# The last expert pair joins the overflow row: both reach their tokens through TensorE, in two parts

## What is computed

```python
pg = softmax(t @ w_rg + b_rg); p_top, g_idx = top_k(pg, 1)          # one group of four
pe_top, e_idx = top_k(softmax(logits of that group), 2)             # two experts of it
w = p_top * pe_top / sum(pe_top)
act = silu(t @ w_gate[e]) * (t @ w_up[e])
y = sum over the two experts e of w[e] * (act @ w_down[e])
x = x + gate * y                                                    # gate: context or latent
```

## Time and profile before

| | us |
|---|---|
| median of 3 runs (lowest, highest) | 1567.03 (1565.42, 1567.63) |
| profiled execution | 1564.47 |
| its span | 1562.7 |
| TensorE busy | 1432.7 |
| VectorE busy | 765.5 |
| ScalarE busy | 324.1 |
| mean granted TensorE clock | 0.962 of full |

### The profile page before, as it was taken

One profiled execution on the slowest core, in us unless ns is written; L12 is line 12 of the kernel. 1 busy time (PEld: TensorE's weight loads), 2 busy tenths in 40 slices (PEclk: granted clock), 3 DMA queues, 4 the chain that ended last, 5 costly groups with the idle time before them and its releaser, 6 DMA issues. The chain is left out here.

```text
span 1562.7 us, 17939 instructions
## 1 busy us (share of the span) xinstructions
PE 1432.7 (92%) x6537; PEld 740.9 (47%) x6537; DVE 765.5 (49%) x1849; ACT 324.1 (21%) x705; POOL 85.7 (5%) x97
## 2 busy tenths in 40 slices
PE   5998998999688999899999999989998998989975
PEld 2335535444255443366666666445443446454432
DVE  1324205553566544576666666036545455156434
ACT  1105304111223111421111111032112125031101
POOL 0000010000210001000000000010001010100001
PEclk9999999999889999899999999999999999989997
DMA  9989968899895998745555554556998730059995
GB/s 353 386 314 364 387 238 323 334 424 422 321 368 210 418 422 351 263 135 175 174 175 175 175 177 157 212 208 237 422 423 341 301 115 1 0 214 401 423 423 221
DMA packets 152276, 436.84 MB, mean 280 GB/s; under 512 B 6944, under 2 KB 63104, under 8 KB 123136
## 3 DMA queue, kind: packets, MB, share of 16 engines
q1 hardware_dynamic: 136816, 396.93, 66.7%
q10 hardware_dynamic: 11920, 26.24, 4.4%
q0 software_dynamic: 3456, 12.58, 2.3%
HBM read 414.20 MB, written 21.53 MB: 279 GB/s over the span
## 5 line engine op out<-in xcount | busy, mean ns | idle before, releaser
L1001 PE MATMUL bank<-gate_up_weights,hT_gathered 128*64 128x512 f32 (+1 forms) x1280 | 256.4, 601 | 15.4 <-SPq L540 14.5
L839 PE MATMUL bank<-panel,hT 128*128 128x512 f32 x384 | 168.8, 599 | 4.9 <-DMA panel<-in_ret_w_in 4.0
L1001 PEld LDWEIGHTS bank<-gate_up_weights,hT_gathered 128*64 128x64 f32 (+1 forms) x1280 | 82.7, 133 | 181.5 <-issue 181.0
L1015 PE MATMUL bank<-down_weights,actT 128*64 128x512 f32 (+1 forms) x640 | 138.5, 603 | 2.5 <-ACT actT L2144 1.7
L1425 DVE SCALAR_TENSOR_TENSOR ada_sums<-panel,cond_columns,ada_sums 128x384 f32<-128x384 f32 x224 | 121.2, 611 | 0.0
L839 PEld LDWEIGHTS bank<-panel,hT 128*128 128x128 f32 x384 | 73.7, 192 | 94.7 <-issue 89.0
L650 PE MATMUL bank<-panel,hT 128*128 128x512 f32 x240 | 107.6, 607 | 3.4 <-DVE hT L1240 2.5
L986 PE MATMUL bank<-h_hi,P 128*128 128x512 f32 x216 | 94.7, 439 | 2.8 <-DVE h_lo L1614 2.7
L986 PE MATMUL bank<-h_lo,P 128*128 128x512 f32 x216 | 87.8, 406 | 0.0
L650 PE MATMUL bank<-panel,oT 128*128 128x512 f32 x192 | 84.3, 595 | 1.3 <-ACT oT L2053 1.3
L2131 ACT ACTIVATE silu<-bank 128x256 f32<-128x256 f32 x36 | 13.9, 385 | 321.6 <-PE bank L1001 321.6
(11 more groups left out here) (330 smaller groups left out, 1929.1 us busy)
## 6 DMA issues: line engine op xcount, KB each, us to landing
gate_up_weights<-in_gate_up_halves SPq DMA_DIRECT2D x148, 1024.0 KB, 13.6
down_weights<-in_down_rows SPq DMA_DIRECT2D x74, 1024.0 KB, 13.6
panel<-in_w_ada SPq DMA_DIRECT2D x27, 2048.0 KB
panel<-in_w_ada SPq DMA_DIRECT2D x16, 1536.0 KB
ada_panel_third<-in_w_ada SPq DMA_DIRECT2D x9, 2048.0 KB
y_by_slot<-y_rows ACTq DMA_DIRECT2D x32, 512.0 KB, 8.2
panel<-in_ret_w_in SPq DMA_DIRECT2D x16, 1024.0 KB
panel<-in_attn_w_qkv SPq DMA_DIRECT2D x6, 2048.0 KB
```

Of the source, the lines that this page charges most:

```text
L839: last = PE.matmul(ps[t][:], hT[:, k, t * 128:(t + 1) * 128], panel[f % 2][:, k, :], start=k == 0, stop=k == KD - 1)
L1001: last = PE.matmul(ps[2][width * s:width * s + width, :], hg[:, j, k, width * s:width * s + width], gu_ring[w][:, 2 * k // KD, :, k % (KD ...
L1015: last = PE.matmul(ps[6 + half][width * s:width * s + width, :], actT[:, c, width * s:width * s + width], dn_ring[w][:, c, half * 512:half ...
```

## The change

- Row 7 (the last pair) is no longer stored and fetched. Its table of slots times weights is made by `weigh_pair`, transposed by TensorE behind row 7's gate-up, and `hot_table` makes of it the weight of each slot (a sum over tokens) and a 0/1 table of tokens. y is multiplied by the slot's weight in `weighted_row`. The overflow row does the same with its own table.
- y of both rows is split in a high part (ScalarE, rounded to the fp32r type) and a low part (VectorE, the difference), and `pe_last_rows` multiplies each with the 0/1 table in fp32r, summing four products in PSUM.
- Fetches wait for rows 0 to 6 alone. Fetches 1, 3, 5 share one buffer, 2 and 4 another, so fetch 3 waits for take 1, 4 for take 2, 5 for take 3. All six takes stand in `last_row`.
- The first QKV panel has a region of its own; `pe_broadcast` uses transposes; the last adds and norm steps are ordered anew; some semaphores are merged; ScalarE starts a layer only when all sums of the last are done.

The core of the diff:

```diff
     pe_row:
         last.then_inc(sem("row_gateup"), 1)
+        if q == PAIRS - 1:
+            pe.wait_ge(sem("row_weights"), 2 * l + 1)
+            pe_table_T().then_inc(sem("row_PT"), 1)
         if not last_row:
             pe_row_gather(pe, l, q + 1, 0)
         else:
-            pe.wait_ge(sem("unit_weights"), l + 1)
+            pe.wait_ge(sem("row_weights"), 2 * l + 2)
+            pe.wait_ge(sem("row_hot"), 2 * l + 1)
             last = pe_table_T()
...
+    def pe_last_rows(pe, l):
+        pe.wait_ge(sem("row_y_lo"), 3 * l + 1)
+        for t in range(TILES):
+            for half in range(2):
+                o = slice(half * 512, half * 512 + 512)
+                for part in (y_hi7, y_lo7):
+                    PE.matmul(ps[2 * t + half][:], hot7[:, t * 128:(t + 1) * 128], part[:, o],
+                              start=part is y_hi7, stop=False)
+        for t in range(TILES):
+            for half in range(2):
+                o = slice(half * 512, half * 512 + 512)
+                if t == 0:
+                    pe.wait_ge(sem("row_y_lo"), 3 * l + 2 + half)
+                PE.matmul(ps[2 * t + half][:], hot8[:, t * 128:(t + 1) * 128], y_hi8[:, o], start=False, stop=False)
+                PE.matmul(ps[2 * t + half][:], hot8[:, t * 128:(t + 1) * 128], y_lo8[:, o], start=False, stop=True)\
+                    .then_inc(sem("unit_sum"), 1)
...
+        def hot_table(l, q):
+            n = 2 * l + q - (PAIRS - 1) + 1
+            dve.wait_ge(sem("row_PT"), n)
+            step(V.tensor_reduce(slot_weight(q), ps[4][:, 0:T], AX.X, ALU.add))
+            V.tensor_scalar(hots[q - (PAIRS - 1)][:], ps[4][:, 0:T], 0.0, None, ALU.is_gt).then_inc(sem("row_hot"), 1)
...
         def last_row(l):
             n = ROWS * l + PAIRS
-            weigh(0, slice(0, 4), "unit_weights")
+            weigh(0, slice(0, 4), "row_weights")
             dve.wait_ge(sem("row_y"), 2 * n)
             step(V.scalar_tensor_tensor(grow[:], gdiff[:], latent[:, PAIRS:ROWS], moe_gate[:, 0, :], ALU.mult, ALU.add))
+            hot_table(l, PAIRS)
+            take(l, 0)
+            take(l, 1)
+            take(l, 2)
+            dve.wait_ge(sem("row_y_hi"), 3 * l + 1)
+            V.tensor_tensor(y_lo7[:], ybuf[:, 1, :], y_hi7[:].bitcast(F), ALU.subtract).then_inc(sem("row_y_lo"), 1)
             dve.wait_ge(sem("row_silu"), n + 1)
             dve.wait_ge(sem("row_actT"), n)
             V.tensor_tensor(act[:], ps[2][:, FE:2 * FE], silu[:], ALU.mult).then_inc(sem("row_act"), 1)
+            take(l, 3)
+            take(l, 4)
             dve.wait_ge(sem("y_stored0"), 16 * 4 * (l + 1))
+            weighted_row(n, PAIRS, 0, ybuf[:, 0, :])
+            weighted_row(n, PAIRS, 1, ybuf[:, 0, :])
             for half in range(2):
-                take(l, half)
                 o = slice(half * 512, half * 512 + 512)
-                dve.wait_ge(sem("row_down"), 2 * n + half + 1)
-                V.tensor_tensor(ybuf[:, 0, o], ps[6 + half][:], grow[:, o], ALU.mult).then_inc(sem("row_y"), 1)
-            take(l, 2)
-            take(l, 3)
+                dve.wait_ge(sem("row_y_hi"), 3 * l + 2 + half)
+                V.tensor_tensor(y_lo8[:, o], ybuf[:, 0, o], y_hi8[:, o].bitcast(F), ALU.subtract).then_inc(sem("row_y_lo"), 1)
+            take(l, 5)
...
     ScalarE, row:
+            if q == PAIRS:
+                e.wait_ge(sem("y_used"), 2 * TILES * l + 1)
+                e.wait_ge(sem("row_y"), 2 * n)
+                S.activation(y_hi7[:], ybuf[:, 1, :], ACT.Copy).then_inc(sem("row_y_hi"), 1)
             e.wait_ge(sem("row_gateup"), n + 1)
...
     GpSimd, combine:
             pool.wait_ge(sem("y_stored0"), 16 * 4 * (l + 1))
-            pool.wait_ge(sem("y_stored1"), 16 * 4 * (l + 1))
+            pool.wait_ge(sem("y_stored1"), 16 * 3 * (l + 1))
             for i in range(2 * TILES):
-                if i == 4:
-                    pool.wait_ge(sem("y_used"), 2 * TILES * l + 1)
-                elif i == 5:
-                    pool.wait_ge(sem("row_gateup"), ROWS * (l + 1))
+                if i == 1:
+                    pool.wait_ge(sem("row_gateup"), ROWS * l + PAIRS)
+                elif i == 2:
+                    pool.wait_ge(sem("row_hT"), 2 * (ROWS * l + PAIRS) + 2)
+                elif i > 2:
+                    pool.wait_ge(sem("y_used"), 2 * TILES * l + i - 1)
...
     SyncE, start:
-        load_next(f)
+        sp.dma_start(first_qkv[:], qkv_w[0, :, :, 0:512]).then_inc(sem("first_qkv_landed"), 16)
...
     pe_broadcast:
-            last = PE.matmul(ps[bank][:, q * 128:(q + 1) * 128],
-                             mods[:, v * KD + 4 * half + q, c:c + 1].broadcast_to([128, 128]), ident,
-                             start=True, stop=True)
+            last = PE.transpose(ps[bank][:, q * 128:(q + 1) * 128],
+                                mods[:, v * KD + 4 * half + q, c:c + 1].broadcast_to([128, 128]), ident)
...
     attention, squares:
-                    dve.wait_ge(sem("qkv_sb"), 9 * a + 3 * i + t + 1)
+                    dve.wait_ge(sem("qkv_sb"), 9 * a + max(3 * i + t + 1, TILES if l == 0 else 0))
```

More of the change, by code:

```diff
@@ L156, in build_trunk @@
     keep("small_place", [3 * FE])
+    lpart_at = top[0]
     lpart = keep("logit_parts", [T])
@@ L182, in build_trunk @@
     (prob, probT), dn_end = region(("prob", [2, 896]), ("probT", [2, 896]), start=dn2_at)
+    assert dn_end <= dn2_at + 2 * size([2, D])
+    (first_qkv,), dn_end = region(("first_qkv_panel", [KD, 512]), start=dn2_at)
     assert dn_end <= dn2_at + 2 * size([2, D])
@@ L225, in build_trunk @@
     tmp_row = tmp[:].rearrange("p a n -> p (a n)")
-    ytok = [tmp_row, ybuf[:, 1, :], hgt[:], hg_rows[:, 1, :], tmp_row, hg_rows[:, 0, :]]
+    ytok = [tmp_row, hg_rows[:, 1, :], hgt[:], hg_rows[:, 1, :], hgt[:], hg_rows[:, 1, :]]
+    Y_BUFFER = (0, 1, 2, 1, 2, 1)
+    Y_TURN = (1, 3, 2)
+    (hot7,), hot_end = region(("pair_hot", [T], R), start=mix0 + 2 * size([TILES, D]))
+    (hot8,), _ = region(("unit_hot", [T], R), start=lpart_at)
+    hots = (hot7, hot8)
+    (y_lo8, y_lo7), _ = region(("unit_y_lo", [D], R), ("pair_y_lo", [D], R), start=base + size([TILES, D]))
+    (y_hi7,), _ = region(("pair_y_hi", [D], R), start=tmp_at)
+    (y_hi8,), _ = region(("unit_y_hi", [D], R), start=base + size([D]))
     ident, tri, iota = kb[:, 0:128], kb[:, 128:256], kb[:, 256:384]
@@ L262, in build_trunk @@
         kind = l % 3
-        first_panel["mix", l] = len(panels)
+        first_panel["mix", l] = len(panels) - (l == 0)
         prj_base[l] = prj
         if kind == 0:
-            panels += [("attn", l, i) for i in range(5)]
+            panels += [("attn", l, i) for i in range(1 if l == 0 else 0, 5)]
             prj += 5 * TILES
@@ L670, in project_k @@
             for k in range(lo, hi):
-                last = PE.matmul(ps[QKV_BANKS[0][t]][:], hT[:, k, t * 128:(t + 1) * 128], panel[f % 2][:, k, :],
+                last = PE.matmul(ps[QKV_BANKS[0][t]][:], hT[:, k, t * 128:(t + 1) * 128], first_qkv[:, k, :],
                                  start=k == 0, stop=k == KD - 1)
@@ L1164, in _ @@
                                  start=True, stop=True)
-        last.then_inc(sem("normf_ps"), 1)
+        last.then_inc(sem("vectors_ps"), 1)
     def mod_col(v, k, c):
@@ L1732, in row @@
                 o = slice(half * 512, half * 512 + 512)
-                dve.wait_ge(sem("row_down"), 2 * n + half + 1)
-                V.tensor_tensor(ybuf[:, q % 2, o], ps[6 + half][:], grow[:, o], ALU.mult).then_inc(sem("row_y"), 1)
+                if q == PAIRS - 1:
+                    weighted_row(n, q, half, ybuf[:, 1, :])
+                else:
+                    dve.wait_ge(sem("row_down"), 2 * n + half + 1)
+                    V.tensor_tensor(ybuf[:, q % 2, o], ps[6 + half][:], grow[:, o], ALU.mult).then_inc(sem("row_y"), 1)
                 if half == 0 and q < PAIRS:
@@ L1822, in tail @@
                 final(0)
-            take(l, 5)
-            mean_square(n, 1)
-            if l + 1 == depth:
                 units_in(l, 2, 0)
+                mean_square(n, 1)
                 units_in(l, 2, 1)
@@ L2146, in row @@
                 if 1 <= l < depth - 1:
-                    e.wait_ge(sem("unit_PT_sb"), l + 1)
+                    e.wait_ge(sem("gate_rows"), l)
                     e.dma_start(gate_rows.rearrange("v c (k f) -> k (v c) f", f=128), mpan[0:KD, :].rearrange("p (g f) -> p g f", f=128))\
                         .then_inc(sem("gate_rows_stored"), 16)
+                for half in range(2):
+                    o = slice(half * 512, half * 512 + 512)
+                    e.wait_ge(sem("row_y"), 2 * n + half + 1)
+                    S.activation(y_hi8[:, o], ybuf[:, 0, o], ACT.Copy).then_inc(sem("row_y_hi"), 1)
                 return
             row_turned(l, q + 1)
+            if q == PAIRS - 1:
+                return
             e.wait_ge(sem("row_y"), 2 * n + 2)
```

74 lines of the change are left out of this document (47 added, 27 removed).

## The result

| | before | after |
|---|---|---|
| median of 4 runs, us (lowest, highest) | 1566.22 (1563.51, 1567.63) | 1594.24 (1591.58, 1595.98) |
| profiled execution, us | 1564.47 | 1591.58 |
| its span, us | 1562.7 | 1589.8 |
| mean granted TensorE clock | 0.962 | 0.951 |

The account below looks back on a forecast made before the run. TensorE, busy 92% of the span, was taken as the bound, with the change in stretches where it is not fed. Terms 29.4 + 1.0 − 2.1 = +28.3 us gave 1592.8 profiled, 1595.3 median; range 1574 to 1604.

Parts of the forecast that it names:

- U behind T: From overflow row's gate-up matmuls ending (T) to VectorE starting to add its sums (U): 21.8, 19.4, 20.8, 18.0 us.
- Act behind the table and three takes: Overflow row on VectorE: act ends at T+7.4 instead of T+1.0, so down matmuls start 6.3 us later, at T+8.3.
- Fetch 3, then 5: Layer ends: fetch 3 issued T+4.6, landing in 5.2 us; fetch 5 waits for take 3, issued T+11.4.
- Then fetch 5 decides: Layer ends: without the slow clock first sums come at T+16.3, but fetch 5 and take 5, last before U, set U.
- those sums end before U+1.3, so 0: ScalarE's later loads and x-scaling now wait for all sums: costs 0, else up to 1 us a layer.
- Layer 3's weights: Wait for layer 3's weights: one store leaves, three fetches enter; between −1.2 and +2.5 us, taken +1.8.
- End of layer 3: Final norm after U: two takes leave VectorE's path, saving 2.4 us; 8.6 − 2.4 = +6.2.
- Start and broadcasts: Gate broadcasts by transposes, taken −1.5 us, and first QKV panel's earlier load, taken −0.6; together −2.1.
- (a): Second fetches land early, clock stays up: U is T+18.0 everywhere, +20.3 us, about 1587; chance 0.20.
- (b): Last fetch takes 9.7 us in layers 0 to 2, beside panel loads: +35 us, 1602; chance 0.10.
- (c): Overflow row's table built before T, takes 0 to 2 end about T, U near T+13.3: 1561 us; chance 0.07.
- (d): Change hides itself: next layers start on weights, not x, and tails cost little; 1567 to 1575 us; chance 0.08.

Follow-up runs that it names:

- Experiment 4: Changed kernel with VectorE's takes 0, 1 and 2 moved ahead of the overflow row's last table; 1577.3 us, ratio 1.0060 to the kernel before.
- experiment 2: Changed kernel with fetches 3, 4 and 5 given places of their own, waiting for no take, VectorE's order unchanged; 1593.8 us, ratio 1.0159.
- experiment 10: Changed kernel with layer 3's fetches held back until the overflow row's gate-up weights have landed; 1591.4 us, ratio 1.0156.
- experiment 11: Changed kernel with own fetch places, takes 0, 1, then act before the last table, takes 4, 5 in tail, layer 3's fetches held; 1556.7 us, ratio 0.9932.
- experiment 9: Kernel before the change with only the transposed gate broadcasts and the first QKV panel's own region; 1563.4 against 1565.8 us, ratio 0.9984.
- experiment 1: Changed kernel with the overflow row's act ahead of table, takes and y_lo7, and ScalarE's y_hi7 copy behind its actT copy; 1602.7 us, ratio 1.0205.
- experiment 7: Changed kernel with 14 unused matmuls on TensorE behind the last table's transposes; 1600.9 us, ratio 1.0225.

## Why the prediction was right, point by point

| layer | U behind T, forecast | measured | end of layer, forecast | measured |
|---|---|---|---|---|
| 0 | 21.8 | 20.3 | +5.6 | +3.9 |
| 1 | 19.4 | 20.4 | +6.0 | +6.3 |
| 2 | 20.8 | 21.3 | +9.8 | +9.6 |
| 3 | 18.0 | 17.7 | +6.2 | +7.2 |

- **Act behind the table and three takes**: it ended at T+7.2 to 7.7 (forecast 7.4); down product from T+8.4 to 8.9 (8.3), 4.9 to 6.0 us long (5.5 to 7.2). Experiment 4 undoes part of it by order alone (act at T+2.9 to 3.9, fetch 3 over 4 us earlier) and gives 17 us.
- **Fetch 3, then 5**: fetch 3 issued at T+4.6 to 5.0 (4.6) and landed in 5.3 to 5.4 (5.2); fetch 5 issued at T+11.4 to 12.0 (11.4) and landed in 7.3, 6.9, 7.7, 4.3 (9.1, 6.3, 7.7, 5.2). The largest miss is layer 0's landing, which put U 1.5 too late; in layer 1 a later issue and a longer landing made U 1.0 later than forecast. The panels were issued at T+10.8 to 11.2 in layers 0 to 2 (9.8).
- **"Then fetch 5 decides"**: in layers 0 to 2 it does, by half a microsecond over the last product. In layer 3 it does not: take 5 did not wait for its fetch, which landed in 4.3 us and not 5.2, and U is right there (17.7 against 18.0) though the wait named as its cause is absent. The step "those sums end before U+1.3, so 0" for ScalarE's new wait is right for this kernel, but the prediction did not say what covers it; the cover is take 5, and experiment 2, which takes it away, pays for it. A forecast of experiment 2 from the prediction's own words would have failed, as mine did.
- **Layer 3's weights**: +1.8 forecast, row 7 to row 8 +2.5 measured, of which 0.35 may be row 7's transposes; the waits beside experiment 10 show the cause.
- **End of layer 3**: the takes gone from the tail were to save 2.4 us; U to the end went from 14.3 to 13.3 us, only 1.0. The other steps of the tail run on ScalarE and POOL, and the takes stood partly beside them. The same is why moving takes 4 and 5 back in experiment 11 costs little.
- **Start and broadcasts**: -2.1 forecast, -2.4 measured by experiment 9. Row 7's +1.0 has no mark of its own. All that lies outside the ends of the layers and layer 3's weights came to -2.3 us in the two profiles, against 1.0 − 2.1 = −1.1, and 1.6 of it is the T of layer 0, which scatters by more. In layer 1 the broadcasts took 1.96 us each instead of 3.84, and most of it went into waits for the next `w_ada` panel (2.07 and 1.59 us where 0.59 stood before).
- **The rivals**: (a) needed last fetches of 5.2 us, seen only in layer 3, which has no panels; (b) needed 9.7 for the last fetch, which took at most 7.7 in the changed kernel; (c), takes ahead of the table, is not what this kernel does, but experiments 4 and 11 show that its mechanism was real; (d) did not show.

Misses that offset one another (layer 0's landing -1.7 by its end, layer 3's weights and tail +1.7) are part of why the sum came out within 0.3 us. That closeness is luck; the terms are good to about 1.7 us each.

## What to carry to other kernels

Before moving work onto an engine, write down its list at the join of two stages with what each entry waits for, and put the entry that feeds the busiest engine (here act) ahead of everything that only uses up landed data. Do it together with sending the fetches early: alone it made this kernel slower. When two chains end together, shortening one shows nothing; try both at once before dismissing either. Look at what a faster step lets go: here it released panel loads into the path of the fetch that everything waited for. And work that only uses landed data is best put where the engine waits for others, as takes 4 and 5 in the tail.

## What was not expected of the hardware

- **An indirect DMA's issue on GpSimd took 1.86 us instead of 0.94** wherever a take on VectorE ran beside its first 1.05 us: fetch 3 in every layer of the changed kernel and of experiment 1, and in experiment 4 fetch 3 of layers 0 to 2 and fetch 5 of layer 3. Being wholly beside VectorE work does not suffice: fetch 4 of layers 0 to 2 in experiment 4 was issued under `y_lo7` alone, in 0.94. Some issues partly beside such work took 1.2 to 1.3 (experiment 2, two of its last fetches). Nothing was run to isolate it. The Trainium skill (GPSIMD Engine Reference, "Specifications") says that GpSimd's SBUF interfaces are shared with VectorE, with contention for instructions with two SBUF inputs; takes and `y_lo7` both have two, so the takes' rows agree and those of `y_lo7` in experiment 4 do not.
- **The same fetch of 512 KB** landed in 4.3 to 5.4 us with little beside it, 6.9 to 7.7 with panels issued near it (both in the changed kernel), and 8.6 with 7 MB of panels issued just ahead and beside it (experiment 1, layer 0). The fit of the Trainium skill (DMA: Bandwidth & Descriptors, "Anatomy of one DMA — SWDGE (gpsimd) path") weighed in the prediction gives an estimate of 3.2 us; the shortest last fetch in these runs took 4.2 (experiment 7, layer 2).
- **One profile is a coarse ruler for a small term.** T of layer 0 was 398.4 to 402.8 us in eleven profiles of kernels that are the same up to row 8 of layer 0. The 1.6 us by which the changed kernel's T came earlier lies inside that, and says nothing by itself; only experiment 9's repeated runs do.
